# Merging the router, expert and combination phases of a hybrid decoder step into one part, with 18 weight places and the first rows found ahead of the table

## The reference, cut to what matters

```python
x = x + (g_s * ssm_out + g_a * attn_out) @ p['w_out']
h = rms_norm(x, p['g_ffn'])
# router: best of 4 groups, then the best 2 of the 8 experts in it, with weights
order = jnp.argsort(e_assign)            # 1152 assignments sorted by expert
...
def expert_block(args):                  # rows of one expert, padded to a block
    xb, e = args
    return (silu(xb @ w_exp_gate[e]) * (xb @ w_exp_up[e])) @ w_exp_down[e]
...
y = rms_norm(x + sum of each token's two expert rows, weighted, g_final)
```

## Time and profile before

| | |
|---|---|
| runs, us | 1308.66 median, 1303.22, 1314.20 |
| the profiled execution | 1310.04 us, of which the span of the core is 1308.4 |
| PE, DVE, ACT, POOL busy | 1076.5, 409.1, 328.0, 276.0 us |
| read from and written to HBM | 284.26 MB and 25.58 MB |
| experts: first L2082 to last L2126 | 753.3 to 1265.9 us of the span |

### The profile page before, as it was taken

The page is one execution under the profiler, slowest core; times in us unless marked ns, Lnnn a source line. Parts: engine busy times, 40 slices in busy tenths (PEclk is TensorE's granted clock), DMA queues, the critical chain, the costliest instruction groups (busy, mean ns, idle before and its releaser), DMA issues. The chain is left out here.

```text
span 1308.4 us, 18689 instructions
## 1 busy us (share of the span) xinstructions
PE 1076.5 (82%) x6695; PEld 679.5 (52%) x6695; DVE 409.1 (31%) x890; ACT 328.0 (25%) x666; POOL 276.0 (21%) x673
## 2 busy tenths in 40 slices
PE   5999999789977868899997288888888888878750
PEld 5999998566655646677444233333333333333320
DVE  4456347647734553414212600000000100000006
ACT  6422222446622231210012022222221222212212
POOL 0006940588721100000000112121111111111110
PEclk9999999879968878989999599788887888898985
DMA  8322252430056517400401779999999999999916
GB/s 335 128 90 73 92 194 88 137 113 1 6 183 185 179 36 315 173 1 1 153 33 57 297 296 410 403 405 406 410 410 403 408 403 407 401 401 412 409 68 232
DMA packets 75132, 299.36 MB, mean 229 GB/s; under 512 B 12630, under 2 KB 35030, under 8 KB 48566
## 3 DMA queue, kind: packets, MB, share of 16 engines
q1 hardware_dynamic: 65934, 280.16, 55.3%
q0 software_dynamic: 7984, 17.33, 4.0%
q10 hardware_dynamic: 1152, 1.05, 0.2%
HBM read 284.26 MB, written 25.58 MB: 237 GB/s over the span
## 5 line engine op out<-in xcount | busy, mean ns | idle before, releaser
L2082 PE MATMUL ps<-arena,local_experts 128*64 128x512 f32 x1024 | 230.0, 598 | 11.4 <-DMA arena<-in_w_exp 10.5
L353 PE MATMUL ps<-local_project 128*128 128x288 f32 (+4 forms) x1608 | 205.9, 290 | 15.2 <-DVE local_project L491 11.6
L353 PEld LDWEIGHTS ps<-local_project 128*128 128x128 f32 (+1 forms) x1608 | 204.7, 184 | 16.0 <-DVE local_project L392 11.6
L2099 PE MATMUL ps<-arena,local_experts 128*64 128x512 f32 x512 | 166.6, 810 | 21.3 <-ACT local_experts L2121 21.3
L2139 DVE SCALAR_TENSOR_TENSOR local_experts<-local_experts,ps 64x512 f32<-64x512 f32 x32 | 21.7, 679 | 464.4 <-ACT local_experts L2117 464.4
L2082 PEld LDWEIGHTS ps<-arena,local_experts 128*64 128x64 f32 x1024 | 83.1, 138 | 155.4 <-issue 155.4
L2099 PEld LDWEIGHTS ps<-arena,local_experts 128*64 128x64 f32 x512 | 52.6, 184 | 108.7 <-issue 108.7
L2061 PE MATMUL ps<-arena,local_experts 64*128 64x64 f32 x457 | 49.4, 246 | 53.1 <-DVE local_experts L2142 42.5
L2047 POOL TENSOR_TENSOR local_experts<-local_experts 1x1 f32<-1x1 f32 x32 | 5.9, 185 | 391.8 <-ACT local_experts L2126 391.8
L2061 PEld LDWEIGHTS ps<-arena,local_experts 64*128 64x128 f32 x457 | 40.1, 162 | 83.7 <-DVE local_experts L2142 46.9
L2126 ACT ACTIVATE local_experts<-ps 64x512 f32<-64x512 f32 x64 | 37.9, 593 | 178.2 <-PE ps L2099 177.4
(11 more groups left out here) (390 smaller groups left out, 1416.7 us busy)
## 6 DMA issues: line engine op xcount, KB each, us to landing
arena<-in_w_exp SPq DMA_DIRECT2D x192, 1024.0 KB, 20.5
arena<-in_w_rest SPq DMA_DIRECT2D x9, 1024.0 KB, 5.7
local_attention<-in_cache SPq DMA_DIRECT2D x56, 128.0 KB, 2.7
arena<-in_w_wide SPq DMA_DIRECT2D x6, 1040.0 KB, 5.0
arena<-scratch_sig SPq DMA_DIRECT2D x2, 2304.0 KB, 14.0
arena<-in_x SPq DMA_DIRECT2D x2, 2048.0 KB, 11.6
arena<-in_cache SPq DMA_DIRECT2D x32, 128.0 KB, 2.3
arena<-in_cache POOLq DMA_DIRECT2D x32, 128.0 KB, 3.6
```

Source lines behind the costliest of these rows:

```text
L353: mm = pe.matmul(out, stationary(s, k), moving(m, k), start=k == 0 and a == 0, stop=k == KD - 1 and a == 2)
L2082: mm = pe.matmul(c.ps[SLOTS * u:SLOTS * (u + 1), 2 + u, :], XT[:, 4 * half + k], raw[at + 2 * half + u][:, k], start=half == 0 and k == 0, ...
L2099: mm = pe.matmul(c.ps[SLOTS * h:SLOTS * (h + 1), 6 + h, :], HT[:, k], raw[at + 4 + h][:, k], start=k == 0, stop=k == KE - 1)
```

## The change

`merge`, `experts` and `combine` become one phase, `tail`, with one block of instructions per engine and no barrier inside. The three functions now return the parts of each engine, and `tail` strings them together.

There are three sets of six places. SP fills places as they come free during the merge: piece 0 of set 0 at once, 1 and 2 after the attention products, 3, 4, 5 of set 0 and 0, 1 of set 1 after the last projection, eight more after the last `w_out` product, piece 4 of set 2 after the last norm, and piece 5 of set 2 when table and block numbers are ready. Then it goes on with block 3. Refills of down come one block later in SP's order than those of gate and up.

The rows of blocks 0 and 1 are found from the ranks of the first two experts alone, with three new DVE instructions and ten new matmuls, before the rest of the table is worked out. POOL stores the last tile of `h` itself and then gathers these two blocks. The table's own matmuls (`table_tensor`) now stand on PE after gate and up of block 0.

Blocks 0 to 29 are written out, with fixed experts, places and table columns. Only the last pair or pairs run in a loop. PE's order is new: the transposition of hidden rows stands between the two halves of the next block's gate and up, and down of a block comes after gate and up of the next one. Gate and up use two pairs of PSUM banks in turn. The two scatters to nowhere at the start are gone, and so are the 1x1 POOL instructions in written-out blocks.

```diff
 ... merge, SP, after the last h row
-            for p in (0, 1, 2, 3, 4, 6, 7, 8, 9, 5):
-                if p == 5:
-                    sp.wait_ge(m_ready, 1)
-                sp.dma_start(c.ring[p], ...)
-            sp.wait_ge(first_in, 16 * RING)
+        piece(0, 0)
+        sp.wait_ge(y_ps, NY)
+        sp.dma_start(w_out[:], c.d["w_out"]).then_inc(wo_in, 16)
+        sp.wait_ge(attn_ps, 16)
+        ... x
+        piece(0, 1)
+        piece(0, 2)
+        sp.wait_ge(proj_ps, 16)
+        for s, p in ((0, 3), (0, 4), (0, 5), (1, 0), (1, 1)):
+            piece(s, p)
+        ... h rows of tiles 0 to 3
+        sp.wait_ge(out_ps, 2 * TILES)
+        for s, p in ((1, 2), (1, 3), (1, 4), (1, 5), (2, 0), (2, 1), (2, 2), (2, 3)):
+            piece(s, p)
+        sp.wait_ge(h_ready, TILES)
+        piece(2, 4)
+        sp.wait_ge(c.table_ready, 1)
+        sp.wait_ge(c.blocks_ready, 1)
+        piece(2, 5)
 ... DVE, after the ranks
+        link(dve.scalar_tensor_tensor(first_rank[:], M[:, 2]...[:, 0:2], -float(SLOTS), c.ps[:, 5, ...], ALU.mult, ALU.add))
+        for q in range(2):
+            dve.tensor_tensor(at_first[:, q], slot, first_rank[:, q], ALU.is_equal).then_inc(first_picked, 1)
 ... seven small instructions on the block counts, as before
+        first_tokens(0)
 ... four on t32, as before
+        first_tokens(1)
 ... the rest of the table; then, moved behind the table's copy out of PSUM,
     the nine on be and bf, with  .then_inc(c.blocks_ready, 1)
 ... experts, POOL
+        for b in range(FIXED):
+            pool.wait_ge(xt_ps, b + 1)
+            gather(b % 2, c.table[:, b + 2, 0:1])
+            pool.wait_ge(y_out, 2 * b + 2)
+            scatter(b % 2, c.table[:, b, 1:2])
 ... experts, SP
+        for b in range(AHEAD, FIXED + 1):
+            if b < FIXED:
+                gate_up(b % AHEAD, lambda p: c.d["w_exp"][b, p], 4 * (b - AHEAD))
+            if b > AHEAD:
+                down((b - 1) % AHEAD, lambda p: c.d["w_exp"][b - 1, p], 2 * (b - 1 - AHEAD))
 ... experts, PE
+        transpose_rows(0, 16)
+        for b in range(FIXED):
+            q = b % 2
+            pe.wait_ge(xt_ready, b + 1)
+            gate_up(q, 0, *fixed_set(b))
+            if b >= 1:
+                turn_hidden(b)
+            gate_up(q, 1, *fixed_set(b))
+            transpose_rows(1 - q, (b + 1) // 2 * 16 + 16)
+            if b == 0:
+                table_tensor(pe)
+            if b == 1:
+                pe.wait_ge(c.table_ready, 1)
+            if b >= 2:
+                pe.wait_ge(y_out, 2 * (b - 1))
+            if b >= 1:
+                down(*fixed_set(b - 1), b)
 ... experts, ACT
+        rows(1)
+        for b in range(FIXED):
+            if b >= 1:
+                hidden(b)
+            gates(b % 2, 4 * b + 4)
+            rows(b + 2)
+            if b >= 1:
+                result((b - 1) % 2, 2 * b, ...)
 ... combine, SP
         sp.dma_start(g[:], c.d["g_final"]).then_inc(g_in, 16)
+        for q in range(2):
+            sp.wait_ge(c.y_stored[q], n * 16)
 ... rows of both choices, as before
```

More of the change, by code:

```diff
@@ L1557, in merge @@
 def merge(nc, c):
-    with ExitStack() as ctx:
[L1561 to L1620, removed]
@@ new lines, in sem @@
+    def sem(name):
+        return c.sem("merge_" + name)
+    local = c.tail_local
+    region = Region(local, 0, LOCAL)
+    small = Region(c.arena, AT_Z4 + 16 * TOK, AT_KT)
+    sig = Region(c.arena, AT_Z4, AT_SSM).take([P, 16, TOK])
+    w_out = Region(c.arena, AT_KT, AT_XM).take([P, KD, D])
+    late = Region(local, 0, 3072)
+    w_glu = region.take([P, 4, D])
+    w_ssm = region.take([P, 4, D])
+    c.x2 = x = Region(c.arena, AT_XM, AT_X2_END).take([P, TILES, D])
+    h = late.take([P, 2, D])
@@ new lines, in merge @@
+    hT = late.take([P, KD, P])
+    w_attn = Region(c.arena, AT_X2_END, AT_LOCAL).take([P, 4, D])
+    glu = Region(local, region.pos, LOCAL).take([P, 4, TOK])
+    y = region.take([NCH, CH, SW])
+    route = Region(local, 13312, LOCAL)
+    tmp = region.take([P, 2, 2, 512])
+    yT = region.take([P, 4, TOK])
+    g_ffn = small.take([P, D])
+    w_route = small.take([P, KD, 36])
+    b_route = small.take([P, 36])
+    c.X_rows = small.take([SLOTS, 2, D])
+    c.table = small.take([SLOTS, TABLE, 2], I32)
@@ new lines, in merge @@
+    c.blocks = small.take([1, BLOCKS + 3], I32)
+    c.token = small.take([SLOTS, 2, 1], I32)
+    at_z = Region(c.arena, AT_Z4, AT_Z4 + 5 * 2048)
+    at_out = Region(c.arena, AT_KT, AT_XM)
+    at_attn = Region(c.arena, AT_X2_END, AT_LOCAL)
+    at_glu = Region(local, 3072, 3072 + 6 * 2048)
+    over_z = [at_z.take([P, 4, 512]) for _ in range(5)]
+    over_out = [at_out.take([P, 4, 512]) for _ in range(4)]
+    over_attn = [at_attn.take([P, 4, 512]) for _ in range(2)]
+    over_glu = [at_glu.take([P, 4, 512]) for _ in range(6)]
@@ new lines, in merge @@
+    pick = route.take([P, TILES])
+    M = route.take([P, 3, TILES, 32])
+    nb = route.take([P, 4, 32])
+    dest = route.take([P, 2, TILES])
+    reached = route.take([P, 2, TILES, TABLE + 1])
+    in_block = route.take([P, 2, TILES])
+    numbers = route.take([P, 2, TILES, TABLE, 2])
+    at_slot = route.take([P, 2, TILES, SLOTS])
+    be = route.take([1, BLOCKS - N_EXP, 32])
+    bf = route.take([1, BLOCKS + 3])
+    sig_in, wg_in, ws_in, wa_in, wo_in, x_in, rt_in = (
+        sem("sig_in"), sem("wg_in"), sem("ws_in"), sem("wa_in"), sem("wo_in"), sem("m_x_in"), sem("rt_in"))
@@ L1632, in _ @@
[L1632 to L1644, removed]
-            for p in (0, 1, 2, 3, 4, 6, 7, 8, 9, 5):
-                if p == 5:
-                    sp.wait_ge(m_ready, 1)
-                sp.dma_start(c.ring[p], c.d["w_exp"][p // PIECES, p % PIECES]).then_inc(first_in, 16)
-            sp.wait_ge(first_in, 16 * RING)
+            merge_sync(sp)
@@ L1652, in _ @@
+            n = experts_sync(sp)
+            combine_sync(sp, n)
+        @block.gpsimd
+        def _(pool):
+            merge_gpsimd(pool)
+            experts_gpsimd(pool)
         @block.tensor
         def _(pe):
[L1654 to L1698, removed]
-                    for k in range(4):
-                        mm = pe.matmul(c.ps[:, 2 * e + u % 2, 0:HALF], w_glu[:, k, (4 * e + j) * P:(4 * e + j + 1) * P],
-                                       yT[:, k, t], start=k == 0, stop=k == 3)
-                    mm.then_inc(glu_ps, 1)
@@ L1703, in _ @@
-            pe.wait_ge(glu_done, 8)
-            pe.wait_ge(ws_in, 16)
-            for u in range(16):
-                m, t = u // 2, slice(u % 2 * HALF, (u % 2 + 1) * HALF)
-                if u >= 2:
-                    pe.wait_ge(proj_done, u - 1)
-                for k in range(4):
-                    mm = pe.matmul(c.ps[:, 4 + u % 2, 0:HALF], w_ssm[:, k, m * P:(m + 1) * P], glu[:, k, t],
-                                   start=k == 0, stop=k == 3)
-                mm.then_inc(proj_ps, 1)
@@ L1749, in _ @@
-            mm.then_inc(rank_ps, 1)
-            for j in range(2):
-                pe.wait_ge(pick_ready, j + 1)
-                for i in range(TILES):
-                    mm = pe.matmul(c.ps[0:SLOTS, 6, 0:2 * TABLE], at_slot[0:ROWS[i], j, i],
-                                   numbers[0:ROWS[i], j, i].rearrange("p b o -> p (b o)"),
-                                   start=j == 0 and i == 0, stop=j == 1 and i == TILES - 1)
-            mm.then_inc(table_ps, 1)
+            merge_tensor(pe)
@@ L2238, in build @@
         c.gate = low.take([P, TILES, 24])
+        c.w1_at = low.pos
         c.w1 = low.take([P, 2, 8, P])
@@ L2245, in build @@
         c.wt = low.take([P, 2, TILES])
-        over_z = Region(c.arena, AT_Z4, AT_KT)
-        c.ring = [over_z.take([P, 4, 512]) for _ in range(PIECES)]
-        c.table = over_z.take([SLOTS, TABLE, 2], I32)
-        c.blocks = over_z.take([1, BLOCKS + 2], I32)
-        over_w_out = Region(c.arena, AT_KT, AT_XM)
-        c.ring += [over_w_out.take([P, 4, 512]) for _ in range(4)]
-        over_attn = Region(c.arena, AT_X2_END, AT_LOCAL)
-        c.ring += [over_attn.take([P, 4, 512]) for _ in range(2)]
         c.pw = Region(c.arena, AT_Z4, AT_Z).take([P, 2, 9, ST])
@@ L2271, in build @@
         attn = ExitStack()
-        for phase in (project, ssm_build, prompt, sample, merge, experts, combine):
+        for phase in (project, ssm_build, prompt, sample, tail):
             if phase is prompt:
@@ L2277, in build @@
                 attn.close()
-            if phase is not combine:
+            if phase is not tail:
                 nc.clear_and_free_semaphores(taken)
```

1045 lines of the change are left out of this document (608 added, 437 removed).

## The result

The changed kernel took 1323.12 us (median of 9, 1317.54 to 1327.97), the kernel before 1305.82 (9 runs): a ratio of 1.0127, interval 1.0099 to 1.0155. It is 17 us (1.3%) slower, clear of the noise. 1288 was forecast, with a range of 1272 to 1305. The profiled execution took 1322.32, its span is 1320.6.

A forecast was written before the change was run, and what follows sets the result against it. Weight transfers on full DMA engines were taken to bound the expert stage. (a) to (e) save 32.0 us, (f) costs 10.7: 21.3 less than the profiled 1310.04, about 1288 as median; range 1272 to 1305.

The forecast's parts named there:

- (f): POOL's in-order queue: gather waits behind an earlier block's scatter, 16.1 us a turn, 10.7 us more in all.
- ring: Expert blocks: result copy, scatter, gather, row transposition and down, each waiting for the one before; forecast 16.1 us a turn.
- Rival C: POOL's queue: gather queues behind the scatter, 7.9 us, with full clock surcharge; turn 17.4, time 1327; chance 0.10.
- (c): Tail of the experts: only block 31's down waits for the last weights, 8.9 us instead of 12.8, 3.9 less.
- (a): Start of the experts: SP's refills restart at 752.9 instead of 759.22, 6.2 us earlier.
- (b): Start of the experts: seventeen weight pieces instead of twelve are in before refills restart, 13.8 us less.
- (d): End seam without barrier: row loads issued 0.2 instead of 7.1 us after the last scatter, 6.9 less.
- (e): End seam: `g_final`, 0.5 MB formerly ahead of the row loads, is in long before; 1.2 us less.
- A: Expert stage: the ring stays slack and transfers bound the stage throughout; 1277 us; chance 0.30.
- D: Early rows bring nothing, refills still wait for block numbers, and fetching written-out blocks loses 3 us; 1297 us; chance 0.15.

The follow-up runs named there:

- e3: Changed kernel, but POOL, after waiting for the earlier block's result, issues the gather first and the scatter second; 1280.9 us, ratio 0.9821.
- e1: Changed kernel, but POOL issues the gather ahead of the earlier block's scatter and without waiting for the result; 1282.03 us, ratio 0.9827.
- e4: Changed kernel with six more unused matmuls on PE per written-out block from the third on, ahead of the wait for gathered rows; 1283.07 us, ratio 0.9856.
- e7: Changed kernel with four chained memsets on POOL between the scatter and the next gather; 1353.65 us, ratio 1.0347.
- e5: e1, with block 3's gate and up refilled as places come free; only piece 5 of set 2 waits for the table; 1273.77 us, ratio 0.9745.
- e6: e1, with five pieces of set 2 held back until table and block numbers are ready, so twelve lie ready; 1292.32 us, ratio 0.988.

## Why the prediction was wrong

The failed step is **(f)**, and of it the size. The mechanism, POOL's queue as a ring, was the forecast's, but its turn was put at 16.1 and is 17.54. PE's end comes out by the forecast's own terms: block 0's down ended at 758.1 instead of 763.0 (-4.9, of which 4.5 came before the ranks), 29 turns by 1.44 more (+41.8), a shorter block 30 in the loop (13.65, -2.45), the last block +0.35: 34.8 later than 1251.4, and the last copy starts at 1286.02. The terms of a turn, the measured ones as means over the 29 turns of the timeline:

| us | forecast | measured |
|---|---|---|
| copy of the result to scatter | 2.1 | 2.02 |
| scatter to gather | 1.23 | 1.23 |
| gather until the transposition of its rows starts | 7.2 | 7.88 |
| transposition and down | 4.55 + 1.0 for the clock | 6.41 |
| one turn | 16.1 | 17.54 |

Two terms make up the 1.44:

- **The gather** was taken at 7.2: +0.7. There it starts 1.94 us behind a scatter, here 1.23, and the forecast took the short distance together with the landing of the long one. Rival C had this, with 7.9, on the ground that it may queue behind the scatter. e3 shows that the second place is what costs: with the order turned round the gather takes 7.4 and the scatter 8.0 instead of 7.0. The forecast's own reason for 7.2, that gathers don't care for the length of the weight queue, held (8.2 in the changed kernel with pieces landing after 10 us, 8.0 in e1 with 30) and was beside the point: what stood ahead of it was its partner in the same queue.
- **The clock** was taken at about two thirds of its surcharge (1.0 of 1.55), a little over the middle between two ends: +0.86. But the wait for the rows stands ahead of transposition and down in nearly every block (30 waits), so the case was the upper end and even beyond it: 1.86 on average, 1.55 to 1.7 in 20 of the 29 turns and 2.7 to 3.3 in seven. e4 prices the clock alone at 40 us in all. The two feed each other: with e3's ring 2 us shorter the waits were shorter and the clock was 0.94.

With both at their upper ends, as in rival C, the ring was 17.4 and the time 1327, against 1323.12. It had been given 0.10. What spoke against it, that gathers would be faster once the DMA engines were not full, was wrong here: at a DMA share of 0.93 to 0.96 the gather still took 8.2. e7 shows 7.4 at a share of 0.89 and 2.71 us behind the scatter, but the kernel before has 7.3 with full engines (1.02) and 1.94, so the distance is enough to explain it.

Of the rest of the sum all but (c) held, as far as the runs without the ring show:

- **(a)** 6.2 forecast, 6.6 measured from the ranks to where SP goes on. e5 shows that an earlier restart is worth nearly its full length.
- **(b)** 13.8 forecast, 13.1 measured in the stream of weights and 12.0 over the span from the table on (e6 against e1, one execution each). The page "DMA: Bandwidth & Descriptors" of the Trainium skill (Anatomy of one DMA) gives its fit of 2.0 us plus bytes over 436e3 per us for transfers issued from GpSimd; an estimate from it is 12.0. The weights here are SP's, and they came at 2.77 a piece in both runs, as the rows said.
- **(c)** failed by 8 us, hidden in the changed kernel by the ring. In e1 the last piece lands at 1238.0 and the row loads start at 1254.85, 16.8 later and not 8.9. The forecast had only down of block 31 behind the last weights. But block 30's down had just begun then, after a wait of 2.7 for unused rows and at the low clock.
- **(d)** 6.9 forecast, 7.05 measured (10.26 to 3.21). **(e)** 1.2 forecast; from row loads to the end 29.35 instead of 31.5, so 2.1, in which the rest is not told apart.
- **A** needed a ring of 15.74 or less. e1, which has none, ends at 1282 and not at A's 1277; from the table to the end it takes 531.0 against 523.5 of the forecast, and (c) is about that difference. **D**: no fetch of code shows as a wait of PE, the early rows did what they should; it didn't happen.

## What to carry to other kernels

When a result is moved a step later, follow the queue of the engine that stores it. If this engine also fetches, each fetch stands behind the store of an earlier step. With the result a step later, that store waits for a result that is only just being made, and the fetch waits with it. Put the fetch ahead of the wait for the result; here these few lines are worth 41 us. Where a wait stands just ahead of matmuls in each turn of a ring, take the clock's whole surcharge, not a share of it; here it was 1.86 us a turn where 1.0 was taken. And take a landing time from a row with the same distance to its neighbour in the queue.

## What was not expected of the hardware

- Of a scatter and a gather of 256 KB issued 1.23 us apart from POOL, the second takes up to 1 us longer than it would as the first: gather 8.2 and scatter 7.0 in one order (changed kernel), 7.4 and 8.0 in the other (e3). With the DMA engines full the second lands 9.2 us after the first was issued, 1.94 apart (7.3, kernel before) or 1.23 apart (8.0, e1; 8.0, e3): the 0.7 us that the shorter distance seems to save come back in the landing.
- Six matmuls without use in a wait of 3.6 us raised the granted clock from 0.88 to 0.99, and took 40 us off the kernel.
- A piece of 1 MB costs 2.77 us in the stream of the kernel before, of e1 and of e6 alike. In e1 PE takes 15.97 us a block while six pieces come in 16.6: it eats a stock of seventeen, and the stage still ends with the weights. In the changed kernel PE was slower than that, 17.54, and set the end itself.
